# Where a projection's engines cut its next weights: ahead of the work it carries, or behind the first piece of it

## The reference

```python
# first block
rq, rk, rv, rg, dq, dk, dv = split(rmsnorm(x) @ w_in)
ret  = silu(rg) * rmsnorm(retention(rq, rk, rv))
diff = rmsnorm(diff_attention(dq, dk, dv, lam))
x = x + concat(ret, diff) @ w_out
x = x + peer(rmsnorm(x), peer_wq, peer_subkeys, peer_u, peer_v)
x = rmsnorm(x)
# second block
q, k, v, qi, ki, wi, z_a, u_b, z_b, gates = split(rms_norm(x) @ w_in_2)
a = attention(q, k, v, 128 keys of top index score) * silu(z_a)
b = (pool(u_b) @ pool_w) * pool_scale * silu(z_b)
g = sigmoid(gates + merge_bias)
y = g[0] * (a @ w_branch_a) + g[1] * (b @ w_branch_b)
x = x + y @ w_out_2
```

## Time and profile before

| what | value |
|---|---|
| time, median of 3 runs | 1953.15 us (1952.82 to 1953.66) |
| the profiled execution: its time | 1951.86 us |
| its span, first to last instruction | 1950.5 us |
| PE busy | 1939.5 us, 99% of the span |
| DVE, ACT, POOL busy | 1209.6, 728.4, 956.7 us |
| granted TensorE clock | 1.000 |

### The profile page before, as it was taken

One profiled execution on the slowest core, in us unless ns is written; L12 is line 12 of the kernel. 1 busy time (PEld: TensorE's weight loads), 2 busy tenths in 40 slices (PEclk: granted clock), 3 DMA queues, 4 the chain that ended last, 5 costly groups with the idle time before them and its releaser, 6 DMA issues.

```text
span 1950.5 us, 23605 instructions
## 1 busy us (share of the span) xinstructions
PE 1939.5 (99%) x9031; PEld 1587.7 (81%) x9031; DVE 1209.6 (62%) x2160; ACT 728.4 (37%) x1045; POOL 956.7 (49%) x665
## 2 busy tenths in 40 slices
PE   8999999999999999999999999999999999999999
PEld 7777888888888778888888888888888888777887
DVE  4464544599999662222223588888888875896344
ACT  3345543332333343222223333333333335645452
POOL 1000000007878888888871677776787600751110
DMA  7543433246666659666678799999999924332122
GB/s 268 189 139 124 150 123 110 64 145 144 146 146 146 134 127 267 145 145 146 145 165 278 250 387 363 376 372 352 361 376 355 387 109 103 87 93 59 54 87 86
DMA packets 183792, 375.74 MB, mean 193 GB/s; under 512 B 61889, under 2 KB 101313, under 8 KB 175233
## 3 DMA queue, kind: packets, MB, share of 16 engines
q1 hardware_dynamic: 109264, 277.03, 42.3%
q0 software_dynamic: 69200, 87.06, 17.3%
q10 hardware_dynamic: 5216, 10.16, 1.5%
HBM read 313.17 MB, written 60.97 MB: 192 GB/s over the span
## 4 chain that ended last, share of the span: by engine, by line
PE 96%; DVE 2%; ACT 1%; issue 0%; DMA 0%; ACTq 0%; DVEq 0%
PE bank L1696 36%; PE bank L330 18%; PE bank L332 18%; PE bank L331 18%; PE bank L2391 1%; PE bank L1245 1%; DVE x L1964 1%; PE bank L2371 1%; PE bank L567 1%; PE bank L1574 1%; DVE v_low L1953 1%; PE bank L2380 1%; PE bank L621 0%; PE bank L587 0%; PE bank L632 0%
## 5 line engine op out<-in xcount | busy, mean ns | idle before, releaser
L1528 POOL DMA_INDIRECT gates_scratch<-slot_gate,slot_place x256 | 435.2, 1700 | 243.0 <-DVE slot_place L1483 156.3
L1696 PE MATMUL bank<-xn_low,u_high 128*128 128x512 f32 x1024 | 403.2, 394 | 0.0
L1696 PE MATMUL bank<-xn_high,u_high 128*128 128x512 f32 x1024 | 399.0, 390 | 0.0
L1696 PE MATMUL bank<-xn_high,u_low 128*128 128x512 f32 x1024 | 398.8, 389 | 0.0
L1748 DVE TENSOR_TENSOR u_low<-u_raw,u_high 128x1024 fp32r<-128x1024 f32 x128 | 156.5, 1223 | 284.1 <-ACT u_high L1719 283.7
L330 PE MATMUL bank<-v_high,w_high 128*128 128x512 f32 x768 | 299.0, 389 | 0.3 <-DVE v_low L1953 0.3
L331 PE MATMUL bank<-v_low,w_high 128*128 128x512 f32 x768 | 298.9, 389 | 0.0
L332 PE MATMUL bank<-v_high,w_low 128*128 128x512 f32 x768 | 298.9, 389 | 0.0
L323 DVE TENSOR_TENSOR weights_low<-weights_raw,weights_high 128x1024 fp32r<-128x1024 f32 (+1 forms) x105 | 129.7, 1238 | 195.0 <-ACT weights_high L312 194.9
L1735 ACT ACTIVATE hidden<-bank 128x512 f32<-128x512 f32 x128 | 76.6, 598 | 420.3 <-PE bank L1696 416.3
L1837 POOL DMA_INDIRECT row<-in_peer_v,row_places x128 | 183.7, 1435 | 86.3 <-DVE x L1964 52.8
(11 more groups left out here) (356 smaller groups left out, 3100.1 us busy)
## 6 DMA issues: line engine op xcount, KB each, us to landing
u_raw<-in_peer_u SPq DMA_DIRECT2D x128, 512.0 KB, 4.0
v_raw<-in_peer_v SPq DMA_DIRECT2D x64, 1024.0 KB, 7.7
weights_raw<-in_w_in SPq DMA_DIRECT2D x62, 512.0 KB, 3.7
hidden_scratch<-hidden SPq DMA_DIRECT2D x128, 192.0 KB
hidden_in<-hidden_scratch SPq DMA_DIRECT2D x32, 768.0 KB, 11.9
gates_scratch<-nothing POOLq DMA_DIRECT2D x32, 576.0 KB, 3.0
gate_in<-gates_scratch SPq DMA_DIRECT2D x32, 576.0 KB, 8.4
weights_raw<-in_w_out SPq DMA_DIRECT2D x16, 512.0 KB, 3.8
```

The lines of the kernel that those rows point to most:

```text
L1528: pool.engine.indirect_dma_start(gates, bass.IndirectOffsetOnAxis(p.slot_place[t][:, i:i + 1], 0), p.slot_gate[t][:, i:i + 1], None, compu ...
L1696: step = pe.engine.matmul(m.bank[b][:, :], left[:, k, :], right[:, k, :], start=(done == 0), stop=(done == 3 * KT - 1))
```

## The change

The two helpers cut chunk c + 2 at the start of chunk c only where the projection carries nothing. Where it carries pieces, the cut comes after the first of the chunk's four pieces. Under gate10 and gate11, the part of b comes behind attention's piece, on both engines. TensorE's, POOL's and SP's programs are as before.

```diff
 def project_scalar(m, name, between=None, evict=None):
     g = m.stream.groups[name]
     for c in range(g.chunk, g.end):
-        split_weights_scalar(m, c + 2)
+        if between is None:
+            split_weights_scalar(m, c + 2)
         for i in range(g.n_banks):
             if evict is not None and c == g.end - 1:
                 evict(i)
             if between is not None:
                 between()
+                if i == 0:
+                    split_weights_scalar(m, c + 2)
 
 def project_vector(m, name, between=None, evict=None):
...
-        split_weights_vector(m, c + 2)
+        if between is None:
+            split_weights_vector(m, c + 2)
...
                 between()
+                if i == 0:
+                    split_weights_vector(m, c + 2)
...
-            project_scalar(m, name, others if half == 0 else lambda: (next(parts, None), others()), empty)
+            project_scalar(m, name, others if half == 0 else lambda: (others(), next(parts, None)), empty)
...
-            project_vector(m, f"gate{half}{branch}", others if half == 0 else lambda: (next(parts, None), others()))
+            project_vector(m, f"gate{half}{branch}", others if half == 0 else lambda: (others(), next(parts, None)))
```

## The result

The change made the kernel slower by 0.23%: the ratio is 1.0023, with a 95% interval of 1.0017 to 1.0030. The medians of 16 executions each are 1956.94 us after (1954.33 to 1958.6) and 1952.48 us before (1950.91 to 1953.66). The forecast was 1953.1 with a range up to 1954.9, so it was wrong, and on the slow side. The profiled execution after took 1957.36 us, with a span of 1956.0, 5.5 us more than before's 1950.5, and with a granted TensorE clock of 0.999 over the whole, where before had 1.000.

The account below looks back on a forecast made before the run. TensorE bounds the kernel, busy 1939.5 of 1950.5 us. Terms + 0.6 + 0 + 0 - 0.4 - 0.25 = - 0.05 us gave 1951.8 profiled; the median stood 1.3 higher, so 1953.1 us, range 1951.4 to 1954.9.

Parts of the forecast that it names:

- z_a and q: Cuts moved behind one more round of choosing keys, gate00's tightest: 0 us lost, bound above 0.5.
- rival C: Cut for gate00: POOL's instructions stretch the low halves, up to 0.5 us late, 1953.6 us; chance 0.08.
- gate10: TensorE's turns under attention go sooner: 0.4 us gained in sum; bounds 1.7 gained, 0.5 lost.
- the displaced exponentials: Under gate10, two or three exponentials come 0.5 us late; 0.5 us lost if each stops TensorE.
- ret_gate: First chunk: late high half delays VectorE's second weight and the fourth score, 0.6 us lost; bounds 0 and 1.0.
- wq1: Cuts now behind pieces that wait for the row of scales: 0 us lost, bound above 0.9.
- R: Time VectorE has the row of scales in wq1: 292.86 before, forecast 291.4; chunk 3's cut ends at R + 10.65.
- rival B: Row of scales stays at 292.86, adding 0.9: 1954.0 us, chance 0.12; from R = 296 on, 1957 or above, 0.03.
- branch_a1: TensorE's wait at the output projection's third chunk goes: 0.25 us gained.
- b's parts: Under gate10 and gate11, needed only a projection later, so their place behind attention costs nothing.
- SP's loads: Moved since each waits for a low half; about a chunk and a half of slack, costed at nothing.

Follow-up runs that it names:

- single_cut: Before, with only the cut for gate00's first chunk (under q's third chunk) moved behind the first piece; 1953.6 us, ratio 1.0007.
- only_vector: After, with ScalarE's cut ahead of the pieces again under z_a and q, VectorE's still behind the first; 1953.93 us, ratio 1.0010.
- narrow_pool: After, with GpSimd's pooled branch and scaling of rows on only 16 or 32 of 512 columns, orders unchanged; 1953.6 us, ratio 1.0009.
- gate10_last: Before, with only the cut under gate10's last chunk moved behind the first piece; 1953.43 us, ratio 1.0008.
- ret_gate_behind: Before, with the new order under ret_gate alone; 1952.67 us, ratio 1.0003.
- d_b_ahead: After, with b's parts ahead of attention's piece again; 1956.67 us, ratio 1.0023.
- gains_only: After, with the cut ahead of the pieces again under z_a, q, ret_gate and in gate10's last chunk; 1950.88 us, ratio 0.9994.
- second_round: After, with the cut for gate00's first chunk behind the second piece of q's third chunk; 1958.69 us, ratio 1.0037.
- gains_again: The same kernel as gains_only, measured once more; 1951.03 us, ratio 0.9994.
- a_choice_ahead: After, with the cut ahead of the pieces again under z_a and q alone; 1952.88 us, ratio 1.0007.
- b_choice_behind: Before, with the cut behind the first piece under z_a and q alone; 1955.64 us, ratio 1.0017.
- c_gate10_ahead: After, with the cut ahead of the pieces again under gate10 alone, b's parts still behind; 1955.39 us, ratio 1.0016.

## Why the prediction was wrong

**z_a and q: the step that failed.** The prediction had 0, with 0.5 us above, by the sentences "two idle stretches before the rounds (about 0.7 to 0.9 us, while VectorE waited for the high halves of z_a) are now filled by pieces. That makes 1722.5, just in time". It measured 3.8 us in the profiled execution. The low half had been ready 0.80 us before it was needed and was now ready 2.17 us behind that (1723.86 + 1.92 against 1723.61), 3.0 us worse. Four things went into it:

- The round itself, 1.5 us, was right: `single_cut` moved the cut by 1.43.
- Of the head start of 0.7 to 0.9 us less than half came. It was read from VectorE's idle stretches as if only VectorE's order changed. But these stretches were waits for the high half, and the same edit moved the high half behind ScalarE's piece. Of three stretches (2.7, 2.7 and 1.0 us in before) the first two stayed, at 3.6 and 2.6 us, and only the third was filled; in sum they shrank by some 0.25. `only_vector` shows the cause: with ScalarE's order old, the wait falls to 0.48 us.
- GpSimd's stretching was the largest error. It was bounded at 0.5 us, by one row of 1.65. A later cut meets another part of GpSimd's work: 1.92 stood in the place of 1.22, 0.7 us, and the six cuts before it took 10.1 us in the place of 8.9, another 1.2, handed on from cut to cut on an engine that waits for nothing. The rival C had the right place and mechanism, and the size of one cut's excess. `narrow_pool` shows that without the stretching the wait is gone.
- The price of a wait was counted at its length. A wait of 2.1 us in TensorE can bring its clock down to 1.2 GHz for some 3 us behind it, 1.6 us more. The prediction has no term for this.

The 3.0 us are thus 1.5 + 0.7 + 1.2, less some 0.4 from idle time and from instructions ahead of these.

**gate10: right in its parts, wrong in its sum.** The gain at the first turn was 0.43 as chained, a later turn gave it back, and with the small gains around it gate01 and gate10's first three chunks won 0.5 in sum, where the prediction had 0.4. The loss was in the sentence on the displaced exponentials, which had them 0.5 us late and costing 0.5 at most. Under the last chunk what was displaced was a bias behind a low half behind a high half behind an exponential, and it cost 1.4 us, in `gate10_last` too, where nothing else is moved. This is the same oversight as above: the cut became part of a chain across two engines.

**ret_gate: right.** 0.6 us, each step of the chain within 0.05 us, and the same in the profile of `ret_gate_behind`.

**wq1: right, its row by luck.** There was no wait, and from R on the chain holds: the cut of chunk 3 is through at 301.2, which is R + 10.65. But R came 0.85 us sooner than forecast by a shorter transfer, and only 0.7 us of the 1.4 that the new order should bring. With before's 7.9 us for the transfer R would be 292.1 and the cuts ready at 302.8 and 308.5; TensorE, 0.7 us late from ret_gate, needed them near 303.6 and 309.1. So by the chain there was no wait either way, and rival B's price did not fall due.

**branch_a1: right.** The wait went; 0.3 us.

**b's parts: right.** Their order can't be told apart (`d_b_ahead`).

The first line of the reasoning, that a change of order can win no more than the waits and can lose more, held: what can win brought 1.2 us at most (`gains_only`), and after as a whole lost 4.5 us between the medians. My chances did not follow it: 0.05 for slower by over 0.2%, with a cut that the sum itself had "just in time".

SP's loads, costed at nothing, were right: TensorE waits for a load at the start of the program alone.

Left open: which executions get the clock's fall, and why a wait of 1.4 us was followed by it under gate10 in some profiles and under gate00 (`single_cut`) in none of 11 executions.

## What to carry to other kernels

An idle stretch counts as slack only if what ends it stays where it is: before filling it, ask whether the same edit moves the instruction that it waits for, here the high half on the other engine. On an engine that waits for nothing every delay is handed on to the end of the stretch, so sum the stretchings of all its instructions, not one; and a forecast of "just in time" is a good chance of a wait. Price a wait of TensorE at its length and, for waits such as these of 1.4 us and more, up to 1.6 us for the clock. Move work behind a piece per place and not per helper: the same edit won under gate01, under gate10's first chunks and under branch_a1, and lost under z_a and q, under gate10's last chunk and in ret_gate.

## What the runs showed of the hardware

I had not expected so short a wait to bring the clock down in an engine that is 99% busy. By the runs, with the longest waits of each profiled execution and the number of executions whose mean clock is given as under 1.000 (it has three decimals; half speed for less than some 2 us of the span would not show in it):

| kernel | longest waits of TensorE behind a low half or a score | executions under 1.000 |
|---|---|---|
| before, beside the experiments | none | 0 of 102 |
| gains_only, gains_again | none | 0 of 22 |
| ret_gate_behind | 0.4 | 0 of 11 |
| single_cut | 1.4 at gate00 | 0 of 11 |
| gate10_last | 1.4 at gate10 | 2 of 11 |
| a_choice_ahead | 1.4 at gate10 | 2 of 11 |
| narrow_pool | 1.4 at gate10 | 4 of 11 |
| only_vector | 0.5 at gate00 and 1.4 at gate10 | 2 of 11 |
| b_choice_behind | 2.1 at gate00 | 6 of 11 |
| c_gate10_ahead | 2.0 at gate00 | 7 of 11 |
| d_b_ahead | 2.1 and 1.4 | 6 of 11 |
| after | 2.1 and 1.4 | 10 of 16 |
| second_round | 3.5 and 1.4 | 5 of 5 |

The longer the wait, the more of the executions show the fall, and it costs about the same whichever wait it follows: 1.6 us at gate00 in after, 1.4 in `second_round`, 1.6 under gate10 in `narrow_pool`. Behind which wait it came only the profiled executions tell; that of `d_b_ahead` has one behind each, with a mean clock of 0.998. After has four executions at 0.998, and they are its four slowest (1957.7 to 1958.6). So the fall also widens the spread: after's 16 executions lie 4.3 us apart, where the kernels without any fall lie 1.3 (`single_cut`) to 2.9 us (`ret_gate_behind`) apart.

The stretch by GpSimd does not fall on all of VectorE's instructions. In after, between 1680 and 1726, the cuts (two SBUF inputs) took 1.72 us where 1.22 is usual, while a round's MAX8 and MATCH_REPLACE8 over 512 columns took 0.69 and 0.68 in both kernels. Two inputs are not the only case, though: a TENSOR_SCALAR over 128x384, with one input, took 1.44 us at 1716.51 in after (1.46 in before) and 0.36 us at 1713.04 in `narrow_pool`.
